# Norm sums and gate logits of a float32 transformer trunk: from float32 matmuls to rounded ones on split operands

## The reference

```python
def rmsnorm(x, g):
    xf = x * lax.rsqrt(jnp.mean(x * x, axis=-1, keepdims=True) + EPS)
    return xf * g

for i in range(2):
    h = rmsnorm(x, mix_norm[i])
    x = x + (swa_sink_attention(h, ...) if i == 0 else gla(h, ...))
    x = x + conv_ffn(rmsnorm(x, ffn_norm[i]), ...)
return rmsnorm(x, final_norm)

def gla(h, w_in, w_gate, b_gate, ...):      # the start of it
    proj = h @ w_in
    q, k, v, g, ga = ...                    # ga: the last 16 columns
    gk = log_sigmoid(ga @ w_gate + b_gate) / 16
```

## Time and profile before

| | |
|---|---|
| Median of 3 runs | 1130.38 us (1130.28 to 1130.58) |
| Span of the profiled execution | 1127.7 us |
| Around the span, up to the median | 2.7 us |
| PE busy | 1106.2 us, 98% |
| DVE, ACT, POOL busy | 578.1, 484.9, 160.9 us |
| Mean granted TensorE clock | 0.997 of full |

### The profile page before, as it was taken

How to read it: one execution, slowest core, us unless ns; L and a number is a source line. 1 busy time by engine, 2 the same in 40 slices (tenths; PEclk the granted TensorE clock), 3 DMA queues, 4 the chain that set the end, 5 groups by cost and what they waited for, 6 DMA issues and landing times.

```text
span 1127.7 us, 14060 instructions
## 1 busy us (share of the span) xinstructions
PE 1106.2 (98%) x5162; PEld 904.4 (80%) x5162; DVE 578.1 (51%) x734; ACT 484.9 (43%) x707; POOL 160.9 (14%) x123
## 2 busy tenths in 40 slices
PE   6999999999999999999999999999999999999996
PEld 4888778888888888887788888778888888888886
DVE  4588566455555543234354556765555555542214
ACT  6366554445544432222652345454545444431211
POOL 6100021111111110001021221121111111110001
PEclk9999999999999999999999999999999999999998
DMA  6511122322223332221223211222222232333222
GB/s 192 162 65 57 44 100 90 103 93 93 93 97 105 110 103 94 86 95 57 77 84 94 83 43 67 76 95 94 93 93 93 103 102 93 107 103 103 81 73 75
DMA packets 31622, 103.48 MB, mean 92 GB/s; under 512 B 3873, under 2 KB 8641, under 8 KB 31586
## 3 DMA queue, kind: packets, MB, share of 16 engines
q1 hardware_dynamic: 27680, 100.68, 26.8%
q10 hardware_dynamic: 3906, 2.31, 1.1%
HBM read 99.56 MB, written 2.88 MB: 91 GB/s over the span
## 4 chain that ended last, share of the span: by engine, by line
PE 89%; DVE 5%; ACT 3%; DMA 1%; POOL 1%; issue 1%; SPq 0%; DVEq 0%; POOLq 0%
PE PS L308 79%; DVE WL L999 2%; PE PS L355 1%; PE PS L629 1%; PE PS L408 1%; POOL SS L1343 1%; ACT WH L671 1%; PE PS L426 1%; DVE X L1024 1%; ACT SQ L701 1%; PE PS L416 1%; DMA X<-xT 1%; PE PS L540 1%; PE PS L572 0%; PE PS L559 0%
## 5 line engine op out<-in xcount | busy, mean ns | idle before, releaser
L308 PE MATMUL PS<-XH,WH 128*128 128x512 f32 x992 | 393.8, 397 | 9.4 <-DVE XL L1017 9.3
L308 PE MATMUL PS<-XH,WL 128*128 128x512 f32 x992 | 386.9, 390 | 0.0
L308 PE MATMUL PS<-XL,WH 128*128 128x512 f32 x992 | 386.6, 390 | 0.0
L999 DVE TENSOR_TENSOR WL<-WRAW,WH 128x1024 fp32r<-128x1024 f32 (+1 forms) x169 | 229.1, 1356 | 245.3 <-ACT WH L740 72.1
L308 PEld LDWEIGHTS PS<-XH,WH 128*128 128x128 f32 x992 | 186.6, 188 | 52.7 <-issue 11.8
L308 PEld LDWEIGHTS PS<-XL,WH 128*128 128x128 f32 x992 | 186.8, 188 | 39.3 <-issue 1.7
L308 PEld LDWEIGHTS PS<-XH,WL 128*128 128x128 f32 x992 | 186.5, 188 | 39.6
L1353 POOL TENSOR_TENSOR CV<-CV,R 128x512 f32<-128x512 f32 x44 | 70.6, 1604 | 416.8 <-ACT CV L717 416.8
L308 PE MATMUL PS<-AH,WL 128*128 128x512 f32 x308 | 121.4, 394 | 0.0
L308 PE MATMUL PS<-AH,WH 128*128 128x512 f32 x308 | 121.4, 394 | 0.0
L308 PE MATMUL PS<-AL,WH 128*128 128x512 f32 x308 | 121.4, 394 | 0.0
(11 more groups left out here) (204 smaller groups left out, 1206.8 us busy)
## 6 DMA issues: line engine op xcount, KB each, us to landing
WRAW<-w_up SPq DMA_DIRECT2D x88, 512.0 KB, 3.3
WRAW<-w_down SPq DMA_DIRECT2D x32, 704.0 KB, 4.1
WRAW<-w_bin SPq DMA_DIRECT2D x24, 512.0 KB, 3.3
WRAW<-w_qkv SPq DMA_DIRECT2D x11, 512.0 KB, 4.7
WRAW<-w_o SPq DMA_DIRECT2D x7, 512.0 KB, 3.4
WRAW<-w_bo SPq DMA_DIRECT2D x7, 512.0 KB, 3.3
X<-xT SPq DMA_DIRECT2D x4, 512.0 KB, 6.7
out<-X SPq DMA_DIRECT2D x5, 256.0 KB, 2.2
```

The costliest lines, as they stand in the source:

```text
L308: last = mm(PS[:, bank], w[:, c:c + P], x[:, kb], start=start and n == 0 and w is wh and x is hi, stop=stop and n == len(kbs) - 1 and w is wl)
L999: tt(WL[:, s, 0:k * P], WRAW[:, s, 0:k * P], WH[:, s, 0:k * P].bitcast(F32), ALU.subtract)\
```

## The change

`mean_square` becomes two float32r matmuls with rounded ones `ONESR`: one on `SSH`, the rounded `SS`, one on `SSL`, the rest `SS - SSH`. ACT writes `SSH` at the head of `std`, DVE writes `SSL` at the head of `inverse_rms`. `gate_logits` becomes one float32r matmul over 128 partitions: `GAT` holds the gate rows rounded at partitions 0, 32 and 96 and their rest at 64, `WGR` the rounded weights at 0, 32 and 64 and their rest at 96. For this DVE makes one product, four copies and one difference; ACT issues three more loads; POOL sets all of `WG` and `GAT`, copies two more parts of `GA`, and writes `WGR`.

```diff
             def mean_square(st):
-                pe.wait_ge(ss_ready, KT_D * (st + 1))
-                mm(PS[:, B4], ONES[:], SS[:], start=True, stop=True).then_inc(ms_done, 1)
+                if st == 0:
+                    pe.wait_ge(onesr_ready, 1)
+                pe.wait_ge(ssl_ready, st + 1)
+                mm(PS[:, B4], ONESR[:], SSH[:], start=True, stop=False)
+                mm(PS[:, B4], ONESR[:], SSL[:], start=False, stop=True).then_inc(ms_done, 1)
...
                 if t == 0:
                     pe.wait_ge(ga_ready, 1)
+                    pe.wait_ge(wgr_ready, 2)
                 if t >= 2:
                     pe.wait_ge(gk_ready, t - 1)
-                mm(PS[:, B6 + t % 2], GAT[0:LO + RANK, t * P:(t + 1) * P], WG[0:LO + RANK, :],
-                   start=True, stop=True).then_inc(z_done, 1)
+                mm(PS[:, B6 + t % 2], GAT[:, t * P:(t + 1) * P], WGR[:], start=True, stop=True).then_inc(z_done, 1)
...
             def std(st):
+                act.wait_ge(ss_ready, KT_D * (st + 1))
+                nc.scalar.copy(SSH[:], SS[:]).then_inc(ssh_ready, 1)
                 act.wait_ge(ms_done, st + 1)
...
+            act.wait_ge(ones_set, 1)
+            nc.scalar.copy(ONESR[:], ONES[:]).then_inc(onesr_ready, 1)
...
-                             (WG[LO:LO + RANK, :], w_gate[0:RANK]), (GARAW[:], w_ga)):
+                             (WG[LO:LO + RANK, :], w_gate[0:RANK]), (WG[2 * LO:2 * LO + RANK, :], w_gate[0:RANK]),
+                             (WG[3 * LO:3 * LO + RANK, :], w_gate[0:RANK]),
+                             (WG[3 * LO + RANK:3 * LO + RANK + 1, :], w_gate[RANK:RANK + 1]), (GARAW[:], w_ga)):
                 act.dma_start(dst, src).then_inc(consts, 16)
...
+            def square_lo(st):
+                dve.wait_ge(ssh_ready, st + 1)
+                tt(SSL[:], SS[:], SSH[:].bitcast(F32), ALU.subtract).then_inc(ssl_ready, 1)
+
             def inverse_rms(st):
+                square_lo(st)
                 dve.wait_ge(std_ready, st + 1)
...
-            for first in (0, LO):
+            link(tt(KS[:, 0], PS[:, B5], R[:], ALU.mult))
+            for first in GA_ROWS:
                 rows = slice(first, first + RANK)
-                last = tt(GAT[rows, :], PS[rows, B5], R[rows], ALU.mult)
-            last.then_inc(ga_ready, 1)
+                nc.vector.tensor_copy(GAT[rows, :], KS[rows, 0]).then_inc(gah_ready, 1)
+            dve.wait_ge(gah_ready, 4)
+            rows = slice(2 * LO, 2 * LO + RANK)
+            tt(GAT[rows, :], KS[rows, 0], GAT[rows, :].bitcast(F32), ALU.subtract).then_inc(ga_ready, 1)
...
-            link(nc.gpsimd.memset(WG[0:LO, :], 0.0))
+            link(nc.gpsimd.memset(WG[:], 0.0))
...
             link(nc.gpsimd.tensor_copy(GA[:, :, 0:RANK], GARAW[:]))
+            link(nc.gpsimd.tensor_copy(GA[:, :, 2 * LO:2 * LO + RANK], GARAW[:]))
+            link(nc.gpsimd.tensor_copy(GA[:, :, 3 * LO:3 * LO + RANK], GARAW[:]))
...
+            nc.gpsimd.tensor_copy(WGR[:], WG[:]).then_inc(wgr_ready, 1)
+            pool.wait_ge(wgr_ready, 1)
+            low = slice(3 * LO, 4 * LO)
+            nc.gpsimd.tensor_tensor(WGR[low, :], WG[low, :], WGR[low, :].bitcast(F32), ALU.subtract).then_inc(wgr_ready, 1)
+            pool.wait_ge(wgr_ready, 2)
...
-            nc.gpsimd.memset(GAT[0:32, :], 1.0).then_inc(small_set, 2)
+            nc.gpsimd.memset(GAT[:].bitcast(F32), 1.0).then_inc(small_set, 2)
```

More of the change, by code:

```diff
@@ L99, in trunk @@
         ONES = place("ONES", [P, P])
-        CONSTS = 11
+        CONSTS = 14
+        ONESR = place("ONESR", [P, P], F32R)
         IDENT = place("IDENT", [P, P])
@@ L110, in trunk @@
         WG = place("WG", [P, BH * HK])
+        WGR = place("WGR", [P, BH * HK], F32R)
         GARAW = place("GARAW", [P, KT_D, RANK])
@@ L168, in trunk @@
         KS = place("KS", [P, 2, T])
-        GAT = place("GAT", [P, T])
+        GAT = place("GAT", [P, T], F32R)
         fifth_raw_b = nc.alloc_sbuf_tensor_at("FIFTH_RAW_B", [P, D], F32, offset=vtt_at)
@@ L178, in trunk @@
         KUT = place("KUT", [P, 4, P], at=ga_at + 4 * 2 * 4 * P)
-        assert ga_at + 8 * KT_D * P <= nc.sbuf_usable_end
+        GA_ROWS = (0, LO, 2 * LO, 3 * LO)
+        SSH = place("SSH", [P, T], F32R, at=ga_at + 4 * KT_D * P)
+        SSL = place("SSL", [P, T], F32R, at=ga_at + 4 * KT_D * P + 4 * T)
+        assert max(ga_at + 8 * KT_D * P, ga_at + 4 * KT_D * P + 8 * T) <= nc.sbuf_usable_end
         PS = ctx.enter_context(nc.psum_tensor("PS", [P, 8, T], F32))
@@ L194, in trunk @@
         sq_ready, ss_ready = sem("sq_ready"), sem("ss_ready")
+        ssh_ready, ssl_ready, onesr_ready = sem("ssh_ready"), sem("ssl_ready"), sem("onesr_ready")
+        gah_ready, wgr_ready = sem("gah_ready"), sem("wgr_ready")
         ms_done, std_ready, r_ready = sem("ms_done"), sem("std_ready"), sem("r_ready")
```

## The result

The changed kernel takes 1135.9 us in the median of five runs (1135.35 to 1137.2), the kernel before 1130.38 (1129.34 to 1130.58): 5.5 us more, a ratio of 1.0053 with a 95% interval of 1.0041 to 1.0065. The forecast was 1133.4 in a range of 1131.6 to 1135.6. The direction is right, the time lies above the range by 0.3 us, and the added time is nearly twice the 3.0 us of the forecast.

What follows compares the result with a forecast made beforehand. PE, busy 98% of the span, was taken as the bound, already waiting for `SS` at the sums. Norm sums +5.1 and logits -2.1 gave +3.0 us, loads 0: 1133.4 us, range 1131.6 to 1135.6.

Steps and rivals of the forecast that it cites:

- The waits of the sums: Four norm sums: PE waits for cast and difference, shorter matmuls included; +0.96 and three times +1.37, +5.1 us in all.
- The cover by DVE's weight difference: Second to fourth norm sums: ACT's 0.62 us cast lies under DVE's weight difference and costs nothing.
- ACT's table load: Before the norm's square root: the 1.28 us load now follows the cast and stays hidden, by 0.3 us at the first sum.
- The logits: Gate logits: four rounded matmuls replace four float32 pairs, gaining 2.1 us, bounds nothing and 3.2.
- the third waits for `GK`: Gate logits: the third logit still waits for DVE's first `GK`, moving only from 548.49 to 547.43.
- the bounds of nothing and 0.69: `GAT` preparation on DVE: each 16x512 copy takes between nothing and 0.69 us; hidden by 2.4 us even at 0.69.
- Loads and small sets: Start and idle stretches: three more constant loads, wider memsets, GpSimd work; taken as 0, upper bound 0.2 us for sets.
- the clock among the rivals: Clock falls in PE's longer waits at the sums: 1134.8 us with one such place, 1136.2 with two; chance 0.10.
- The rival's price of 1.4 us per place: After a norm sum: seven matmuls run at the lower clock, each losing 0.20 us, 1.4 us in all; chance 0.10.
- its time for two places: Clock falling after two norm sums: 1136.2 us in all; chance 0.10.
- the waits stay short: Argument against a clock fall at the norm sums, where PE would idle about 2.4 us (first) and 2.1 (second).
- The base: Whole kernel: profiled span 1127.7 us plus 2.7 around it, the median of 1130.4, to which +3.0 was added.

Runs made afterwards that it cites:

- gates_only: The kernel before with only the gate logits changed, norm sums still float32 matmuls on `SS`: 1127.59 us, ratio 0.9979.
- filler: The changed kernel plus seven matmuls nobody reads, before PE's wait at the second and fourth norm sums: 1132.6 us, ratio 1.0024.
- wait_f32: The changed kernel with each norm sum again one float32 matmul on `SS`, still waiting for `SSL`: 1137.71 us, ratio 1.0069.
- after: The changed kernel itself, against the kernel before, in its first set of runs: 1135.9 us; its profiled execution has a span of 1134.1 us.
- norms_only: The kernel before with only the norm sums changed, logits still float32: 1137.87 us, ratio 1.0072.
- changed_again: The changed kernel, unaltered, timed once more: 1135.44 us, ratio 1.0049.
- moved: The changed kernel with the second, third and fourth norm sums later in PE's list, the first unmoved: 1127.79 us, ratio 0.9976.
- undo_2_4: The changed kernel with the second and fourth norm sums as in the kernel before: 1130.8 us, ratio 1.0006.
- moved_first32: The changed kernel with the last three norm sums later in PE's list and the first again float32 on `SS`: 1125.58 us, ratio 0.9960.

## Why the prediction was wrong, point by point

**The waits of the sums** were right: +0.99, +1.31, +1.29 and +1.29 us in the trace at full clock, 4.9 in all against the 5.1 of the sum. (The second: 169.56 + 0.57 - 167.82, less the 1.01 by which all is late there.) The pair holds PE for 0.57 us at full clock (534.28 to 534.85) against 0.58. The cover by DVE's weight difference held at three places, and ACT's table load stayed hidden.

**The logits** were right: 2.14 us in the trace, 2.3 in the time of gates_only, against 2.1; the third waits for `GK` as told. `GAT` was ready at 542.37, 3.4 us before PE used it at 545.77. The four copies took 1.77 us, 0.44 each, between the bounds of nothing and 0.69. Since nobody waited for them, their price did not change the time. By the Trainium skill's double rate (VectorE: DVE Perf Modes, "The perf-mode tier table") they would take 0.35 each, an estimate from half of the 0.69; the measured 0.44 is longer than that, but nearer to it than to my bound.

**Loads and small sets** cost nothing: the transposes begin at 41.92 in the chain instead of 40.93, 0.99 us late like everything there.

**The step that failed** is the one that put the clock among the rivals with 0.10 and let the sum go by waits alone: the sum had nothing for the half clock. In the trace the clock falls after two of the four sums and earlier at the very end: 0.42 + 1.12 = 1.54 us at the second (the pair, then the stream), 1.62 at the fourth, 0.5 at the end, 3.7 in all. filler, which differs from the changed kernel only in what PE does while it waits, shows that it is the idleness: 2.8 us come back. wait_f32 shows that it is not the kind of matmul.

The rival's price of 1.4 us per place was near (1.54 and 1.62), and its time for two places, 1136.2, is 0.3 us above what was measured; the range, which ended at 1135.6, did not reach to it. That it came so near is in part luck: it has 2.8 us for the clock where the trace has 3.7, and its base is 0.9 too high (below), and the two cancel. I had argued that "the waits stay short" and named no row with a wait of about 2 us that kept its clock. The kernel before has none: behind its first matmul PE's longest wait was 1.1 us, so its trace could not tell that 1.9 to 2.5 us would cost nothing. The Trainium skill's rule that idleness throttles the array (TensorE: Matmul & The Clock Gate, Part 1) stood against the change, and the trace agrees: the clock is 0.50 of full after the second and fourth sums.

**Which wait costs the clock** is only partly known. Of the profiled executions in which PE idles for `SSL` without a filler, the clock fell behind the second sum in four of four (after, norms_only, wait_f32, changed_again; a wait of 1.9 us), behind the fourth in two of the same four (after, wait_f32; 1.9 us), behind the first in four of seven (changed_again, filler, moved, undo_2_4, but not after, norms_only, wait_f32; up to 2.5 us), and behind the third in none of six (1.5 us). At the second sum PE was idle twice within a few microseconds, for 0.75 to 1.44 us before the unit and then before the sum, with three matmuls between. That may be why it is hit each time, but it is not needed: ahead of the fourth sum PE's stream has no such wait in any of these traces, and there and at the first sum the clock fell all the same. The longest wait, 2.5 us at the first sum, kept its clock in the trace of the changed kernel and lost it in that of changed_again, which is the same program. What picks the place in an execution stays open; I did not find a quantity in the traces that decides it.

**The base** was off by 0.9 us between the profiled execution and the median; the forecast was made against the median, so the misfit shows as 6.4 us between traces and 5.5 between medians.

## What to carry to other kernels

A shorter instruction on the bounding engine gains nothing if it needs two new steps that this engine waits for: count the steps in series first, and put the instruction where other work covers them. Here the same split costs 5 us of waits and up to 3.7 of clock in the old place, and at three of the four sums it gains 1.2 to 1.6 us half a unit to one unit later. Where a change gives PE waits of about 2 us, as here, put the half clock after them into the sum or at least into the range, and test it with a few matmuls whose result nobody reads.

## What the runs showed of the hardware that I had not expected

The clock can fall after PE has gone back to work: at the fourth sum the matmuls were 0.23 us apart from 762.75 on and 0.43 from 763.78 to 766.34. The executions of one program differ in which of the waits cost them the clock (after and changed_again). A fall cost 1.54 us at the second sum and 1.62 at the fourth in the changed kernel's trace; at the first it cost 1.2, since part of it lies under a short wait of PE there (the transposes begin at 43.14 in changed_again against 41.92). The kernels with such a wait spread by 1.6 to 3.2 us between executions and moved_first32 by 0.5, but the falls are not all of that: the kernel before spreads over 2.9 us in one set of 27 executions, whose mean clocks all are 0.996 or 0.997. Matmuls whose result nobody reads made a kernel 2.8 us faster.
